# Feed-forward blocks in woven order, and the first differential pair weighed one lane step later

## The reference

```python
# differential attention, one block of queries
p = jax.nn.softmax(sc, axis=-1)
a = (p[:, 0] - lam * p[:, 1]).astype(v.dtype)
return jnp.einsum('bhqk,bkhd->bqhd', a, v)
```

## Time and profile before

| | |
|---|---|
| median of 3 runs | 2029.14 us |
| the profiled execution: its time | 2028.63 us |
| its span, first to last instruction | 2026.8 us |
| PE busy | 2015.5 us (99%) |
| DVE busy | 1391.4 us (69%) |
| ACT busy | 1022.1 us (50%) |
| granted clock of PE | 0.999 |
| L1661, all `tokens` products: share of the chain that ended last | 65% |
| L1678 and L1675, `wide` units: share of it | 18% and 9% |

### The profile page before, as it was taken

How to read it: one execution, slowest core, us unless ns; L and a number is a source line. 1 busy time by engine, 2 the same in 40 slices (tenths; PEclk the granted TensorE clock), 3 DMA queues, 4 the chain that set the end, 5 groups by cost and what they waited for, 6 DMA issues and landing times.

```text
span 2026.8 us, 24812 instructions
## 1 busy us (share of the span) xinstructions
PE 2015.5 (99%) x10220; PEld 1701.7 (84%) x10220; DVE 1391.4 (69%) x1657; ACT 1022.1 (50%) x1218; POOL 88.5 (4%) x128
## 2 busy tenths in 40 slices
PE   9999999999999999999999999999999999999998
PEld 7888878888888888878888888888888888888887
DVE  6655697775757676787675667657767577577675
ACT  6444568453445345667453356654534466545331
POOL 1001010000010001100100000000100000000000
PEclk9999999999999999999999999999999999999999
DMA  9655544465656555444566574654655555555552
GB/s 335 212 187 169 174 164 146 162 207 195 193 182 224 192 179 192 159 147 162 195 209 197 167 230 136 207 167 170 243 196 188 189 174 187 167 186 202 193 187 83
DMA packets 225568, 377.64 MB, mean 186 GB/s; under 512 B 6624, under 2 KB 113248, under 8 KB 225456
## 3 DMA queue, kind: packets, MB, share of 16 engines
q1 hardware_dynamic: 221472, 362.64, 54.3%
q0 software_dynamic: 3984, 13.43, 2.0%
HBM read 374.99 MB, written 1.05 MB: 186 GB/s over the span
## 4 chain that ended last, share of the span: by engine, by line
PE 99%; DVE 1%; issue 0%; ACT 0%; DVEq 0%; POOL 0%; POOLq 0%
PE pb L1661 65%; PE pb L1678 18%; PE pb L1675 9%; PE pb L1687 2%; PE pb L1733 1%; PE pb L1812 1%; PE pb L1799 0%; PE pb L1811 0%; DVE wl L2119 0%; PE pb L1791 0%; PE pb L1650 0%; PE pb L1654 0%; PE pb L1692 0%; PE pb L1652 0%; PE pb L1819 0%
## 5 line engine op out<-in xcount | busy, mean ns | idle before, releaser
L1889 ACT ACTIVATE wh<-raw 128x2048 fp32r<-128x2048 f32 (+2 forms) x347 | 653.8, 1884 | 620.7 <-PE pb L1661 289.5
L2119 DVE TENSOR_TENSOR wl<-raw,wh 128x2048 fp32r<-128x2048 f32 (+2 forms) x345 | 774.7, 2253 | 149.0 <-ACT wh L1889 148.5
L1661 PE MATMUL pb<-wh,x 128*128 128x512 f32 (+1 forms) x2144 | 651.3, 386 | 0.0
L1661 PEld LDWEIGHTS pb<-wh,x 128*128 128x128 f32 x2144 | 400.8, 188 | 77.8
L1661 PE MATMUL pb<-wl,x 128*128 128x512 f32 (+1 forms) x1072 | 421.0, 393 | 0.0
L1678 PE MATMUL pb<-x,wh 128*128 128x512 f32 x1568 | 381.2, 392 | 0.0
L1678 PEld LDWEIGHTS pb<-x,wh 128*128 128x128 f32 x1568 | 287.6, 188 | 55.2
L1661 PE MATMUL pb<-wl,mh 128*128 128x512 f32 (+1 forms) x740 | 255.6, 391 | 0.0
L1661 PE MATMUL pb<-wh,ml 128*128 128x512 f32 (+1 forms) x740 | 253.7, 388 | 0.0
L1661 PE MATMUL pb<-wh,mh 128*128 128x512 f32 (+1 forms) x740 | 253.6, 388 | 0.0
L1661 PEld LDWEIGHTS pb<-wl,x 128*128 128x128 f32 x1072 | 201.5, 188 | 41.8 <-issue 3.7
(11 more groups left out here) (359 smaller groups left out, 1550.3 us busy)
## 6 DMA issues: line engine op xcount, KB each, us to landing
raw<-in_w_in_dram SPq DMA_DIRECT2D x100, 1024.0 KB, 5.2
raw<-in_w_ff_dram SPq DMA_DIRECT2D x64, 1024.0 KB, 5.4
raw<-in_ffn_w_down_dram SPq DMA_DIRECT2D x44, 1024.0 KB, 5.0
raw<-in_ffn_w_up_dram SPq DMA_DIRECT2D x42, 1024.0 KB, 5.3
raw<-in_ffn_w_gate_dram SPq DMA_DIRECT2D x41, 1024.0 KB, 5.3
raw<-in_w_branch_dram SPq DMA_DIRECT2D x24, 1024.0 KB, 5.0
raw<-in_w_out_dram SPq DMA_DIRECT2D x16, 1024.0 KB, 5.1
raw<-in_w_in_dram SPq DMA_DIRECT2D x4, 832.0 KB, 4.5
```

Source lines behind the costliest of these rows:

```text
L1661: ins = e.matmul(pb[b][:, 0:c1 - c0], x[:, s, cols], w[:, n, c0:c1], start=(it["first"] and n == 0 and q == 0), stop=(it["stop"] and n == ...
L1889: e.activation(hi, raw, ACT.Copy).then_inc(m.high_done, 1)
L2119: e.tensor_tensor(lo, raw, hi.bitcast(F32), ALU.subtract).then_inc(m.low_done, 1)
```

## The change

The feed-forward units become `woven`: both halves of a unit go through their high tiles and then through their low tiles, and the next unit the other way round, so that the blocks of eight are high 0, high 1, low 0, low 1, then low 0, low 1, high 0, high 1. The first item holds three of the four blocks, the second the last. Units on banks 4 to 7 take their first planner step before the unit instead of between the items. The first differential pair of a layer has one more `yield` ahead of `weigh2`.

```diff
+WIDE_ORDER = {False: ((False, 0), (False, 1), (True, 0), (True, 1)),
+              True: ((True, 0), (True, 1), (False, 0), (False, 1))}
...
+    def woven_group(self, key, banks, epi, turned):
+
+        j = self.take(key)
+        self.split(j)
+        need = self.need("X", range(8), [0, 1])
+        if banks[0] >= 4:
+            self.tick()
+        uses = [self.use(b) for b in banks]
+        for i in range(2):
+            if i and banks[0] < 4:
+                self.tick()
+            v = self.pe("woven", j=j, i=i, uses=uses, need=need, turned=turned)
+            epi(i, v["p"], uses[i])
+        self.freed[j] = self.x_free = v["p"]
+        self.tick()
...
-                        self.wide_group((gate, (l,), 0, 8, c0 + c, 256), self.pair(0, side), self.gate_w(q))
-                        self.wide_group((up, (l,), 0, 8, c0 + c, 256), self.pair(1, side), self.up_w(q, slot + 2 * q))
+                        self.woven_group((gate, (l,), 0, 8, c0 + c, 256), self.pair(0, side), self.gate_w(q), False)
+                        self.woven_group((up, (l,), 0, 8, c0 + c, 256), self.pair(1, side), self.up_w(q, slot + 2 * q),
+                                         True)
...
-                    self.wide_group(("w_ff1_2", (l,), 0, 8, n0 + 512 * c + 256 * q, 256), self.pair(n_t % 2, n_t % 4 > 1),
-                                    self.relu_w(q, 4 * c + 2 * q))
+                    self.woven_group(("w_ff1_2", (l,), 0, 8, n0 + 512 * c + 256 * q, 256),
+                                     self.pair(n_t % 2, n_t % 4 > 1), self.relu_w(q, 4 * c + 2 * q), n_t % 2 == 1)
...
         while not self.pin_free or len(self.dv) < 2:
+            yield
+        if f == 0:
             yield
         w = self.side()
         v = self.pe("weigh2", kind="diff", lane=0, f=f, use=w, need=[("evac", uses[0]), ("evac", uses[1])] + self.dv)
...
+        elif k == "woven":
+            hi, lo = m.weights(it["j"])
+            pe.wait_ge(m.low_done, it["j"] + 1)
+            pe.all_ready(it["need"])
+            steps = WIDE_ORDER[it["turned"]]
+            for low, q in steps[0:3] if i == 0 else steps[3:4]:
+                (b, g), c = it["uses"][q], slice(q * P, q * P + P)
+                first = low == it["turned"]
+                if first:
+                    pe.wait_ge(m.evac[b], g)
+                for s in range(8):
+                    if low:
+                        ins = e.matmul(pb[b][:, 0:S], lo[:, s, c], m.xh[:, s, :], start=(first and s == 0),
+                                       stop=(not first and s == 7), skip_group_check=True)
+                    else:
+                        ins = e.matmul(pb[b][:, :], hi[:, s, c], m.x2[:, s, :, :].rearrange("p a s -> p (a s)"),
+                                       start=(first and s == 0), stop=(not first and s == 7), skip_group_check=True)
+            ins.then_inc(m.pe_done, 1)
```

## The result

The changed kernel takes 2035.36 us (median of 9 runs, 2033.6 to 2037.03) against 2028.81 (9 runs of before beside it): ratio 1.003, 95% interval 1.0019 to 1.004. It is slower by 6.5 us where 0.2 were forecast, and outside the range given. The profiled execution took 2035.36 us, its span is 2033.6.

A forecast was written before the change was run, and what follows sets the result against it. TensorE was taken as the bound, busy 2015.5 of 2026.8 us. From the profiled 2028.63, -0.7 (woven order) and +0.9 (later weighting) gave 2028.8; with 0.5 for the median of runs, 2029.3 us, range 2026.3 to 2031.0.

The forecast's parts named there:

- Part 1: Feed-forward units in woven order, 39 pairs: fewer low-to-high steps gain 0.8 us, transposes lose 0.1, net -0.7 us.
- rival 3: Feed-forward units: the weave is worth nothing, by longer low runs or the skill page's rule; 2030.0 us, 10%.
- Part 2: First differential weighting of each layer one lane step later: 1.76 us hole filled, net +0.45 us a layer, +0.9 in two.
- (a): After the query projection PE starts key/value products at once; second key product hands over at 259.67, 2.47 us ahead.
- (d): First MLA score waits 1.7 us for its q copy on ACT, behind a later softmax; gates go on at 279.07.
- Rival 4: Hole before the value products stays because they waited for something else, with `weigh2` on top; 2030.8 us, 8%.
- (b): `weigh2`, now between two gate products, costs 1.0 us of PE time.
- (c): Later differential lane steps move by one, MLA's don't; PE wants the first MLA score at 276.25.
- 0.4 if the softmax starts where it did: Bound on the wait at the first MLA score: 0.4 us if the second pair's softmax is not delayed.
- Rival 1: First MLA score: hole filled and no new wait, the q copy is ready; 2026.7 us, at best 2025.9, 20%.
- (e): After the first MLA score, put-off weight transposes (0.35 us) and two separated stops (0.1 each): +0.45 a layer, +0.9 us.
- Rival 2: ACT's queue delays later pairs, at MLA weightings behind third-pair exponentials, about 1.0 us at two pairs per layer; 2033.3 us, 7%.

The follow-up runs named there:

- the held split: Changed kernel with two table loads less per layer, plus one weight split planned behind the second pair's softmax instead of ahead of it: 2027.7 us.
- the unturned order: Kernel with the weighting in the hole (2024.89 us), woven, but every unit high, high, low, low, none turned: 2026.24 us.

## Why the prediction was wrong

**Part 1, the woven order: right in kind, a little large.** Predicted -0.7 us, measured -0.5, with a pair of 11.11 us as forecast. Runs of 32 low products cost 3.83 us (516.47 to 520.30), 0.96 a block, so rival 3 (nothing gained) falls. Pairs of 11.11 us for 11.13 are the 0.02 a pair that was forecast, 0.8 us in all; 0.1 of it was forecast to be lost at transposes, and what takes back the rest was not looked into. Rival 3 would have followed too from the formula that the prediction took from the Trainium skill's page "TensorE: Matmul & The Clock Gate", section "Back-to-back issue gap"; that section gives it for a single matmul by itself, not for a stream. The rows decide against it, if only by half a microsecond.

**Part 2 (a) to (d): right, to 0.4 us.** (a) First gate product 259.80, predicted 259.67; the hole is gone and 0.17 us stands before the second key product. Rival 4 falls. (b) `weigh2` between gate products cost 0.9 us, predicted 1.0: the lead fell from 2.34 to 1.45. (c) PE wants the first MLA score at 277.93 - 1.31 = 276.62, predicted 276.25. (d) The softmax starts at 268.23, predicted 267.95; the score at 277.93, predicted 277.95, and gates go on at 279.16, predicted 279.07. The wait's mechanism was right and is confirmed by the held split, but the lower bound "0.4 if the softmax starts where it did" was not reachable: the scores themselves come later, and with the split held the wait is 0.5. Rival 1 (no wait) falls. Two sums in the working don't come out, and neither moves the forecast: 9.87 us behind 267.95 is 277.82, not 277.85, and the forecast's own span with both bounds added is 2028.1 to 2030.9, not 2028.0 to 2030.3.

**The step that failed is (e),** "Net per layer 0.55 - 0.1 = +0.45 ... two layers +0.9 us". It closed the account with what the differential lane still owed PE and took ACT's queue as done with at the first MLA pair. Without the fourth wait that sum stands: in the kernel with fewer table loads the products behind the fourth score of layer 1 start 0.85 - 0.33 = 0.52 us later than before, counted from the start of the run, and it takes 2029.32 us. The sum put the fourth score's wait at nothing, without a row for it. But the step moves ACT's work too: squares, logarithms and exponentials of the differential end, four table loads among them, moved against MLA's fourth pair, and ACT stands idle 2.5 us longer ahead of them. What that costs is two waits of 1.96 us, and, where the clock falls behind one, 4.47 - 0.91 - 1.96 = 1.6 us more (0.91 is how much later PE wants the fourth score, 350.91 for 350.00).

**Rival 2 was the right kind at the wrong place.** It had ACT's queue hold later pairs, at 2033.3 us. That this is close to the 2033.6 of the runs in which the clock did not fall is luck: it counted 1.0 us at two pairs in each layer, where one pair waits 1.96. It saw the late work at MLA's weightings, behind the third pair's exponentials, and put the chance at 7% because "PE has been delayed by then". PE had been delayed by 0.91 us, the copy by 2.9. The row that pointed to the right place was in the trace of before: the score at 350.00 behind a copy that ended at 349.95. The half clock stood in no rival.

**Still open.** Why the clock fell behind one wait of 1.96 us in a run and not behind the other: the traces show when, not what decides it. Of the changed kernel 3 runs stand at 2033.6 to 2033.7 us, 5 at 2035.2 to 2035.7 and one at 2037.0; that these are none, one and two falls is read from the steps, from one profile with one fall and from the mean granted clock of each run (0.999 in the three, 0.998 in the six, which can't tell one fall from two). Why DVE is late at the unturned order's own wait (0.6 us) was not looked into either.

## What to carry to other kernels

When a step in a lane is moved, follow every later step of that lane on each engine to its last instruction, and ask at each meeting with another lane how much the consumer had to spare in the trace of before; a place with 0.05 us to spare pays for all of the delay that the consumer does not share (here 1.96 of 2.86 us). To fill a hole, move only the instruction that fits and keep what comes after in phase: the same weighting in the same hole won 3.5 us that way and lost 7 the other. Price a wait that is new on TensorE with what may follow it, not by its own length alone.

## What the runs showed of the hardware

With waits of 1.3 us (two kernels, 22 runs with two or four of them each) the runs of a kernel agree within 0.8 us. With waits of 1.96 us they spread in steps of about 1.7 us, and so do 18 of 84 runs of the kernel before, with its holes of 1.76 us, which stand 1.1 us or more above the median. Of 17 such runs of the kernel before whose mean granted clock is on record, 15 have 0.998; the 58 others beside them have 0.999 or 1.000. The four kernels whose longest wait behind the start is 0.6 us or none (44 runs) agree within 0.9 us each. Not everything fits: one run of the held split, with waits of 0.5 us, stands 1.1 us above its median at 0.999. With 3.0 us most runs stand at the top. Where a profile has the fall, the clock is 0.50 (1.2 GHz) for some 3 us while PE works, and then 1.00 again.

A switch between the logarithm and the exponential on ACT costs the table load of 1.28 us and 0.14 beside it, and in this kernel the order of four activations is worth 2.84 us of ACT in each layer.
